# Joining the gated up product and the down product of the second block's feed-forward in one block

## The reference

```python
def conv_glu(h, w_up, conv_w, conv_b, w_down):
    gate, val = jnp.split(h @ w_up, 2, axis=-1)
    gate = depthwise_conv(gate, conv_w, conv_b)
    return (jax.nn.gelu(gate, approximate=False) * val) @ w_down
...
        ffn_x = conv_glu(modulate(rms_norm_2(x, ffn_pre_norm[l]), mod_x[3], mod_x[4]),
                         w_up[l], ffn_conv_w[l], ffn_conv_b[l], w_down[l])
        x = x + mod_x[5] * rms_norm_2(ffn_x, ffn_post_norm[l])
```

## Time and profile before

| what | value |
|---|---|
| runs: median (lowest to highest), 3 runs | 4364.1 us (4361.16 to 4365.38) |
| profiled execution: span from first to last instruction | 4362.6 us |
| busy share of the span: PE, DVE, ACT, POOL | 89%, 62%, 46%, 22% |
| up product's stage, its first instruction | 3580.2 us |
| down product's stage, its first instruction | 4100.2 us |

### The profile page before, as it was taken

The page is one execution under the profiler, slowest core; times in us unless marked ns, Lnnn a source line. Parts: engine busy times, 40 slices in busy tenths (PEclk is TensorE's granted clock), DMA queues, the critical chain, the costliest instruction groups (busy, mean ns, idle before and its releaser), DMA issues. The chain is left out here.

```text
span 4362.6 us, 58869 instructions
## 1 busy us (share of the span) xinstructions
PE 3863.8 (89%) x22208; PEld 2989.3 (69%) x22208; DVE 2702.1 (62%) x4089; ACT 1997.9 (46%) x3668; POOL 964.3 (22%) x1100
## 2 busy tenths in 40 slices
PE   6989898987999887986789999999787969999898
PEld 5765677876775666765656666677566758888686
DVE  3756577966656477966555555548866655565555
ACT  4544265534554275344434444445543544443344
POOL 0017004610006002600045555500082000111000
PEclk7989899998999998988999999999899989999999
DMA  5100113655100111033100000121003541111243
GB/s 179 39 15 1 64 39 127 220 180 183 39 20 1 45 45 52 2 100 106 29 5 5 10 5 5 47 82 53 7 1 134 179 142 39 39 58 39 97 149 140
DMA packets 211403, 297.09 MB, mean 68 GB/s; under 512 B 74218, under 2 KB 140010, under 8 KB 211124
## 3 DMA queue, kind: packets, MB, share of 16 engines
q1 hardware_dynamic: 210564, 293.14, 20.2%
q0 software_dynamic: 416, 0.05, 0.0%
q10 hardware_dynamic: 144, 0.15, 0.0%
HBM read 262.17 MB, written 31.03 MB: 67 GB/s over the span
## 5 line engine op out<-in xcount | busy, mean ns | idle before, releaser
L513 DVE TENSOR_TENSOR x_low<-buf_a,x_high 128x1280 fp32r<-128x1280 f32 (+4 forms) x384 | 376.5, 980 | 430.9 <-ACT x_high L482 427.5
L539 PE MATMUL ps<-x_high,w_high 128*128 128x512 f32 (+1 forms) x1344 | 496.7, 370 | 94.9 <-DVE w_low L517 88.4
L482 ACT CAST x_high<-buf_a 128x1280 fp32r<-128x1280 f32 (+4 forms) x384 | 327.8, 854 | 534.9 <-PE ps L541 465.1
L540 PE MATMUL ps<-x_low,w_high 128*128 128x512 f32 (+1 forms) x1344 | 484.5, 360 | 0.0
L541 PE MATMUL ps<-x_high,w_low 128*128 128x512 f32 (+1 forms) x1344 | 483.2, 360 | 0.0
L2954 PE MATMUL ps<-w_high,x_high 128*128 128x512 f32 x896 | 363.9, 406 | 91.3 <-DVE w_low L2797 87.6
L539 PEld LDWEIGHTS ps<-x_high,w_high 128*128 128x128 f32 x1344 | 258.3, 192 | 166.8 <-DVE x_low L513 105.5
L2956 PE MATMUL ps<-w_high,x_low 128*128 128x512 f32 x896 | 358.0, 400 | 0.0
L2955 PE MATMUL ps<-w_low,x_high 128*128 128x512 f32 x896 | 358.0, 400 | 0.0
L2797 DVE TENSOR_TENSOR w_low<-w,w_high 128x1024 fp32r<-128x1024 f32 x170 | 208.0, 1224 | 194.5 <-ACT w_high L2910 194.5
L3506 DVE TENSOR_REDUCE mx<-ps 128x1 fp32r<-128x1280 f32 x128 | 190.8, 1491 | 199.7 <-PE ps L3381 199.2
(11 more groups left out here) (444 smaller groups left out, 8952.0 us busy)
## 6 DMA issues: line engine op xcount, KB each, us to landing
w<-in_w_out SPq DMA_DIRECT2D x26, 2048.0 KB, 8.9
w<-in_w_mod SPq DMA_DIRECT2D x24, 2048.0 KB, 9.1
w<-in_w_down SPq DMA_DIRECT2D x15, 2048.0 KB, 7.8
w<-in_w_in SPq DMA_DIRECT2D x26, 1024.0 KB, 5.2
w<-in_w_up SPq DMA_DIRECT2D x22, 1024.0 KB, 7.6
w<-in_w_in SPq DMA_DIRECT2D x6, 2048.0 KB, 8.3
x<-in_x SPq DMA_DIRECT2D x16, 512.0 KB, 9.0
scratch_branches<-buf_b SPq DMA_DIRECT2D x4, 1280.0 KB, 5.5
```

What stands on the lines that cost most here:

```text
L482: act.copy(xh[i % NX][:, 0:s["tn"]], x_of(s)).then_inc(x_high, 1)
L513: dve.tensor_tensor(xl[i % NX][:, 0:s["tn"]], x_of(s), xh[i % NX][:, 0:s["tn"]].bitcast(F32), ALU.subtract).then_inc(x_low, 1)
L539: pe.matmul(g["out"], lhs[0][:, :], rhs[0][:, :], start=(s["kk"] == 0), stop=False)
L540: pe.matmul(g["out"], lhs[0][:, :], rhs[1][:, :], start=False, stop=False)
```

## The change

- **One block.** `K.joined` opens one `nc.Block`, and `K.stage` hands it to both stages. `k.done` inside it only collects the semaphores, and the clearing and the wait of all engines come once, behind the down product. No other pair of stages is joined.
- **The tail moves.** What stood behind the last up step is cut in numbered parts (`last(i)` on DVE and on ACT, kept in an `FfnTail`). `project_normalize` calls part `i` behind the casts and subtractions of its step `i`: part 0 copies the last gates and values, DVE's parts 1 to 6 are the six convolution instructions, ACT's parts 4 and 7 the two gelus. POOL's stream has its multiplications in the same order as before.
- **Waits in their place.** ACT waits before step 0 of the down product until DVE has read the last slice of the up product's input and 20 multiplications are done, and before steps 20 and 21 for multiplication 21 and 22. PE waits in step 0 for the copy out of each bank. SP waits for all 22 multiplications before it loads `gate_row`, `post_row` and the residual tiles, and loads one weight chunk ahead of that wait. `constants` stands behind step 14.
- **Memory and banks.** The up product's operands, `g_raw` and `G` (5 tiles in the first region instead of 9) lie elsewhere, and the banks of the up product are numbered by `BANKS`, so that the down product's buffers and banks are free when it starts.
- **The first pass.** In pass 0 all 8 slices of half 0 come first, then those of half 1, and each of its 16 steps makes its own `w_high` and `w_low`. That is 8 more casts on ACT and 8 more subtractions on DVE. The object `Turned` stands for the stage ahead and does nothing here (`STEPS` is 0).
- **The taps.** DVE's wait for the taps now stands behind the subtractions of step 0.

```diff
+    @contextmanager
+    def joined(self):
+
+        assert self.block is None
+        with self.nc.Block() as block:
+            self.block = block
+            yield
+        self.block = None
+        self.done(self.later)
+        self.later = []
...
     def done(self, sems):
 
+        if self.block is not None:
+            self.later += list(sems)
+            return
         self.nc.clear_and_free_semaphores(list(sems))
         self.nc.all_engine_barrier(sem_only=True)
...
+    BANKS = ((4, 5, 0, 1), (2, 3, 6, 7))
...
+    def ready(self, act, i):
+
+        if i == 0:
+            act.wait_ge(self.x_low, len(self.order))
+            act.wait_ge(self.done, KF - 2)
+        if KF - 2 <= i < KF:
+            act.wait_ge(self.done, i + 1)
+
+    def bank_free(self, pe, bank):
+        b, sub = self.of_bank[bank]
+        pe.wait_ge((self.gate_out, self.value_out)[sub // 2], 4 * (KF // 2 - 1) + 2 * b + sub % 2 + 1)
+
+    def ended(self, sp):
+        sp.wait_ge(self.done, KF)
+        sp.wait_ge(self.k.ws.products, self.end)
...
+    order, after, w_after, group_ready, n = [], [], {}, {}, base
+    for jj in range(NPASS):
+        for a in range(KD * NB):
+            kk, b = divmod(a, NB) if jj else (a % KD, a // KD)
+            fresh = jj == 0 or b == 0
+            w = (order[-1][4] if order else -1) + fresh
+            order.append((jj, kk, b, fresh, w))
...
+            def last(i):
+                if i == 0:
+                    for b in range(NB):
+                        values(NPASS - 1, b)
+                elif i <= 6:
+                    conv(KF - 2 + (i - 1) // 3, (i - 1) % 3)
...
-            dve.wait_ge(taps_in, 64)
-            dve.wait_ge(padded, 2)
...
-                if b == 0:
+                if fresh:
                     dve.wait_ge(w_high, w + 1)
...
+                if x == before.STEPS:
+                    dve.wait_ge(taps_in, 64)
+                    dve.wait_ge(padded, 2)
...
+            def last(i):
+                if i == 0:
+                    for b in range(NB):
+                        gates(NPASS - 1, b)
+                elif i in (4, 7):
+                    gelu(KF - 2 + (i - 4) // 3)
...
-                if i == 1:
+                if i == (14 if after else 1):
                     constants()
                 norms(s["kk"], before[s["g"]])
                 next(parts, None)
+                if after:
+                    after.dve(i)
...
+                    elif s["kk"] == 0 and after:
+                        for half in range(2):
+                            after.bank_free(pe, bank_of[n] + half)
...
+            if after:
+                ws.load_until(sp, first_chunk + 1)
+                after.ended(sp)
             for s in gate_row:
```

More of the change, by code:

```diff
@@ L574, in bank @@
         return 4 + 2 * (n % 2) + half
-    with nc.Block() as block:
+    with k.stage() as block:
         @block.sync
@@ L1997, in ssd_scan, with __init__, ffn_up @@
     k.done(sems)
-def ffn_up(k, XT, G, rooms):
+class FfnTail:
+    BANKS = ((4, 5, 0, 1), (2, 3, 6, 7))
+    def __init__(self, k, order, x_low, gate_out, value_out, done, end):
+        self.k, self.order = k, order
+        self.x_low, self.gate_out, self.value_out, self.done, self.end = x_low, gate_out, value_out, done, end
+        self.of_bank = {bank: (b, sub) for b in range(2) for sub, bank in enumerate(self.BANKS[b])}
+    def ready(self, act, i):
[10 more added lines that the diff above has]
+        sp.wait_ge(self.k.ws.products, self.end)
+def ffn_up(k, XT, G, place, before):
     nc, ps, d, ws = k.nc, k.ps, k.d, k.ws
@@ L2037, in ffn_up @@
                        "dve_chain", "convolved", "activated", "done")
-    with nc.Block() as block:
-        @block.sync
-        def _(sp):
-            for i in range(3):
-                sp.dma_start(taps[:, i, :], d["ffn_conv_w_2"][0, i].rearrange("(c p) -> p c", p=P)).then_inc(taps_in, 16)
-            sp.dma_start(taps[:, 3, :], d["ffn_conv_b_2"][0].rearrange("(c p) -> p c", p=P)).then_inc(taps_in, 16)
-            ws.load_until(sp, ws.taken)
+    tail = FfnTail(k, order, x_low, gate_out, value_out, done, ws.count)
@@ new lines, in _ @@
+            for x, (jj, kk, b, fresh, w) in enumerate(order):
+                pe.wait_ge(w_low, w + 1)
+                pe.wait_ge(x_low, x + 1)
+                for sub in range(4):
+                    if kk == 0 and jj >= 1:
+                        pe.wait_ge((gate_out, value_out)[sub // 2], 4 * (jj - 1) + 2 * b + sub % 2 + 1)
+                    elif kk == 0:
+                        before.bank_free(pe, BANKS[b][sub])
+                    o = ps[:, BANKS[b][sub], :]
+                    c = slice(sub * P, (sub + 1) * P)
+                    pe.matmul(o, wh[w % NW][:, c], xh[x % NX][:, :], start=(kk == 0), stop=False)
+                    pe.matmul(o, wh[w % NW][:, c], xl[x % NX][:, :], start=False, stop=False)
+                    mm = pe.matmul(o, wl[w % NW][:, c], xh[x % NX][:, :], start=False, stop=(kk == KD - 1))
+                    if kk == KD - 1:
+                        mm.then_inc(ws.products, 1)
+                if kk < KD - 1:
+                    mm.then_inc(ws.products, 1)
+                if x < before.STEPS:
+                    before.pe(x)
@@ L2172, in ffn_up, with _ @@
+        @block.sync
+        def _(sp):
+            for i in range(3):
+                sp.dma_start(taps[:, i, :], d["ffn_conv_w_2"][0, i].rearrange("(c p) -> p c", p=P)).then_inc(taps_in, 16)
+            sp.dma_start(taps[:, 3, :], d["ffn_conv_b_2"][0].rearrange("(c p) -> p c", p=P)).then_inc(taps_in, 16)
+            before.sp()
+            ws.load_until(sp, ws.taken)
     k.done(sems)
+    return tail
 def fourier(k, fu, yt, ctx_out, lay, moves):
@@ L2536, in pe, with rooms_free, turned, bank_free @@
             yield
-def project_normalize(k, y, kt, tiles, sizes, xt, mod_cols, gain, lay, gates, post=None, pre=None, stored=None, beside=None):
+class Turned:
+    STEPS, n_tiles = 0, 0
+    def rooms_free(self, act):
+        pass
+    def turned(self, engine, n):
+        pass
+    def bank_free(self, pe, bank):
+        pass
+    def stores_done(self, engine):
+        pass
+    def sp(self):
+        pass
+def project_normalize(k, y, kt, tiles, sizes, xt, mod_cols, gain, lay, gates, post=None, pre=None, stored=None, beside=None,
+                      after=None):
     nc, ps, d, ws = k.nc, k.ps, k.d, k.ws
```

205 lines of the change are left out of this document (97 added, 108 removed).

## The result

The changed kernel takes **4327.6 us** (median of 4 runs, 4326.14 to 4333.44) against 4363.41 for the kernel before (4 runs, 4361.16 to 4365.38). The ratio is 0.9917, with a 95% interval of 0.9903 to 0.9931.

The account below looks back on a forecast made before the run. TensorE, busy 3863.8 of 4362.6 us, was taken as the bound, with holes at the seam and the up product's start. Gains of 16.9 + 2.6 + 2.8 = 22.3 us gave 4341.8 us, range 4337.3 to 4346.1.

Parts of the forecast that it names:

- The hole and the slow clock at the seam: Between up and down product: PE's wait goes, 16.9 us, and the slow matmuls behind it go, 2.6 us.
- The taps: Start of the up product: step 0 runs before the taps land, step 1 is slow again; 2.8 us gained.
- The moved tail: Beside steps 0 to 7 of the down product: the tail's work fits without delaying PE; cost 0.
- SP, `constants`: Down product: loads held behind the multiplications, and `constants` behind step 14, still come in time; cost 0.
- POOL's hold: Down product's first steps: two multiplications hold DVE just behind a `w_low`; taken as 0, otherwise 1.7 us.
- Pass 0: Start of the up product: 8 more casts and 8 more subtractions fit, chain 1.6 us in a 2.80 us step; cost 0.
- The clock did not stay up: Rival, up product between steps 0 and 1: clock stays up, 2.5 us more gained, 4339.3 us; chance 0.2.
- no `w_low` was late: Rival, down product's first steps: late `w_low` by POOL's hold or step 1's copies, 1.7 us, 4343.5; chance 0.1.
- pass 0 was not bound by its weights: Rival, up product's pass 0: steps last as long as their weights' chain, slower, 4372.6 us; chance 0.02.
- the joining joins: Rival denied here: PE still waits at the seam, only the step at the start is gained, 4361.3 us; chance 0.02.
- the upper end of the range: Whole kernel: late `w_low` plus the branch's 1.0 and 1.5 us of spread, given as 4346.1 us.
- The 12 slow matmuls near 3582: Sign at the up product's start: PE has 12 slow matmuls, a rest of 4 us, then 12 more from 3591.

Follow-up runs that it names:

- `changed_not_joined`: The changed kernel in two blocks again, with the tail run at the end of the up product: 4348.67 us, ratio 0.9964 to the kernel before.
- `taps_behind_step0`: The kernel before with only DVE's wait for the taps moved behind step 0's subtractions: 4359.98 us, ratio 0.9992.
- `changed_down_w_416`: The changed kernel with 416 bytes left free between the x and w tiles of the down product: 4334.69 us, one run.
- `pad_32`: The kernel before with 32 bytes more in front of the up product's x operands: 4360.40 us, one run.

## Why the prediction was wrong, and where it was right

- **The hole and the slow clock at the seam: right.** 16.9 + 2.6 = 19.5 us forecast, 19.3 measured (`changed_not_joined`: 16.9 of hole, 2.2 of slow clock, and some scatter). Its steps hold too: the casts ahead of the copies, the banks free in time, no idle time of PE.
- **The taps: right.** 2.8 us forecast, 3.3 measured in the kernel before, 3.0 without the sooner landing. The choice that the clock falls again in a rest of some 4 us was the right one: 3.60 us were enough in the changed kernel, 3.93 in `taps_behind_step0`.
- **The terms costed at nothing.** The moved tail: right; even ahead of `w_low` it costs some 0.4 us. SP, `constants`: right, no wait. POOL's hold: the mechanism came as said (two instructions of DVE held) and fell beside the `w_low`s, not on them. By the Trainium skill, "SBUF — State Buffer", section "SBUF: two separate sides", the lock lasts as long as one instruction; the two held ones came to an end 0.54 and 0.41 us behind POOL's, and nothing speaks against it. The two start as worked out, 14.6 and 26.8 us behind the down product's first matmul (forecast near 4101 and 4113, 14.9 and 26.9 behind its 4086.15). Pass 0: no hole, and 178 matmuls in the window of 40 us.
- **The step that failed** is one that the sum didn't have: the up product's 2112 matmuls were carried over at their old distance of 0.233 us, a term put at nothing without a reason. They take 0.2267, and that is 13.3 us of the up product (13.5 of the stretch). The edit "Memory and banks" was read only for what it makes free, the buffers and banks; as a change to every matmul of the stage it got neither a price nor bounds. The trace of before had the hint. I quoted it, "173 records in 40.00 us" in the one product and 178 in the other, same shape, same clock, no hole in either, and didn't ask why the one costs 3% more. Had I bounded it (0.233 down to 0.227 in 2112 matmuls, 12.7 us), the range would have reached from 4337.3 down to 4324.6 and held the result.
- **The rivals**: none came in the changed kernel. The clock did not stay up, no `w_low` was late, pass 0 was not bound by its weights, and the joining joins. None of them gives 4327.6; the lowest stood at 4339.3.
- **The sums**: the upper end of the range adds up to 4343.5 + 1.0 + 1.5 = 4346.0 where the text has 4346.1, which changes nothing. The 12 slow matmuls near 3582 were some 10: PE was back at 0.23 us within step 0. It didn't matter, since step 1 waited for the taps.

Shown by the runs: what each of the three parts is worth to about half a microsecond, that the places do it and not the banks, that it goes by relative and not by absolute place, and that it slows either product. Only argued: that 256 bytes is the unit. Open: by what mechanism it comes about. In the kernel before, steps that use `x_low0` last 2.81 us on average behind the sixth step, and those with `x_low1` and `x_low2` 2.80 and 2.79, though the latter two have 0 bytes between `x_low` and `w_high`. Most of this fits: 8 of the 12 matmuls of every step read an `x_high`, 416 bytes away, and 8 at 0.2343 us (2.81 / 12, the same as in the down product of `changed_down_w_416`) with 4 at 0.2267 would make 2.78. But in `pad_32` the three kinds last 2.80, 2.79 and 2.81, with the last one, whose `x_low2` is at 0 bytes, the slowest, so the distance of each single matmul's two operands does not tell everything.

## What to carry to other kernels

Where the same matmul, at the same clock and without a hole, comes less often in one stage than in another, the slower stage has a cost of its own; count the records in windows of equal length, since the mean duration of one hardly shows it (389 ns in the fast up product, 394 to 397 in the slow one, from 3700 to 3900). Treat a change of where operands lie as a change to every instruction that reads them, and give it bounds. When tiles of a product follow odd-sized ones, try the layout in which moving and stationary operands keep a distance of a multiple of 256 bytes, and measure it: here it was 13 us for a reordering of tiles, and in earlier stages next to nothing. And put a wait at the first instruction that needs it: moving the taps' wait twice brought 3.3 and then 6.7 us.

## What the runs showed of the hardware that was not expected

- The start-to-start distance of matmuls of 128x128 by 512 in rounded float, at a granted clock of 1.00, depends on where the two operands lie in SBUF relative to each other: 0.2267 us at distances of 0, 512 and 768 bytes, 0.2343 us where all moving tiles were at 416 (`changed_down_w_416`), 0.2332 on average where four of the six were (the kernel before). Loads of weights overlapped in both cases. PSUM banks made no difference (859 and 859, 884 and 884). The Trainium skill, "TensorE: Matmul & The Clock Gate", section "Step-by-step: what each phase is for", says that loading the next tile's weights takes no read bandwidth from the running matmul, as each has a read port of its own. By that one would not expect their places relative to each other to matter; here they cost 3%, and the measurement decides. Whether it is the weight load that disturbs the moving operand's reads, no run shows.
- Moving everything together by 32 bytes made no difference (737.1 and 737.4 us).
- Behind a rest of 3.60 us PE was slow again, at 0.43 us a matmul; the shortest such rest seen before was 4.23 us. How long it stays slow differs: behind its first start in the up product it was back at 0.23 us with the eleventh matmul in the changed kernel, and with the thirteenth in the kernel before.
